# Bias vectors kept in DRAM in 16 copies, read back by eight loads with a step of 511

## The chip, the cores and the metric

The kernel runs on one core of one Trainium2 chip. The metric is the device time of one execution in microseconds (us). All arithmetic is in 32-bit floats; large matrix products are made of three passes over a high and a low part of each operand.

## The reference, cut to what matters

Two transformer blocks follow each other over 256 tokens of width 1024. The first has a mixer of three kinds (differential attention, an RWKV-7 recurrence, attention over a memory) and a mixture of 16 experts. The second has two layers, each with two feed-forward nets of width 2816 around a mixer. In these two layers every attention score gets a bias that depends only on the distance between query and key:

```
bias[h, q, k] = table[bucket(q - k), h]      # 16 heads, masked where q < k
layer 0: heads 0-7 a mixture of dilated windows, heads 8-15 the best keys of an index
layer 1: 16 heads, window of 128, a sink for each head
out = softmax(q k^T / 8 + bias) v
```

So for one head the whole 256 x 256 bias follows from a vector of 512 values: row p of a tile is the vector read from a place that moves by one element for each p (a Toeplitz tile).

## The kernel before, in words

**Weights.** The weights are a stream of slots of 1.5 MB, in the order in which they are used. SyncE (SP) loads each slot in three pieces "a", "b" and "d" of 512 KB into `raw`, which has two slots (L423). ScalarE (ACT) copies a piece to `w_hi` (L536), VectorE (DVE) writes the rest to `w_lo` (L907), and TensorE (PE) multiplies (L1478 to L1480). Piece a or b of slot n may be loaded once slot n-2 has been split, and the order on SP is a(n+1), b(n+1), d(n). ACT and DVE split the pieces in program order among their other work, so a piece that comes late holds what follows it on both engines. All loads of SP use the queue q1.

**Stages.** Slots 0 to 9 are the projections of the first mixer; three slots (OUT0) are its output projection; 64 slots are the experts (`MOE0`); then come a feed-forward net of 22 slots (`FFA0`), the mixer of layer 0 (`HYB0`, attention, three slots `HOUT0`), two feed-forward nets (`FFB0`, `FFC0`), the mixer of layer 1 (`SWA0`, attention, `SOUT0`) and the last net (`FFD0`). Before each of them a norm computes, transposes and splits the activations.

**Bias.** Early on, PE makes two sets of vectors, one for each layer (L1755), and ACT copies them to `vec_sb`, 16 partitions (one for each head) of 2 x 512 floats (L729, semaphore `vec_ready`). GpSimd (POOL) waits until the first mixer's attention has its first scores (L484) and then stores, for each of the two sets, the whole Toeplitz tiles to DRAM: from each of the 16 partitions 128 overlapping rows of 384 floats (L488), 3 MB for each set, to `bias_tiles` (`bias_dram` in the code, shape 2 x 16 x 128 x 384). Before the feed-forward net `FFA0` it loads the first set into `zb`, 128 partitions of 16 x 384 floats (L499); after the attention of layer 0 it loads the second (L514). The waits for `bias_loaded` stand before the attentions that use them. All DMAs of POOL use the queue q0.

```
pool.wait_ge(S_("att_scores"), 1)
for v in range(2):
    row = vec_sb[0:16, v, P - 1:P]
    pool.dma_start(bias_dram[v], bass.AP(row.tensor, row.offset, [list(row.ap[0]), [-1, P], [1, 3 * P]]))
...
pool.dma_start(zb, bias_dram[0].rearrange("h p c -> p h c"))
```

Of the kernel before, what the change touches and what calls it, by code (L numbers as in the profile page):

```python
# [16 lines left out]
F32 = mybir.dt.float32  # L17
# [6 lines left out]
P = 128  # L24
# [68 lines left out]
LAM_INIT = 0.8 - 0.6  # L93
RMS_EPS = 1e-6
TOP_ROUNDS = S // 4 // 8
RW_GN_EPS = 64e-5


def block_program(nc, wstream, x_in, mem_in, pos_in, pos_cols_in, pcol_in, prow_in, smallw_in, const_in, table_in, bias_lookup_in,
                  bias_dram, out):  # L100
    ctx = ExitStack()
    with ctx:
# [5 lines left out]
        def S_(name):  # L108
            if name not in sems:
                sems[name] = ctx.enter_context(nc.semaphore(name))  # L110
            return sems[name]
# [21 lines left out]
        def at(kb, *shape):  # L133

            n = int(np.prod(shape))
            o = int(kb * 256)
            assert o + n <= arena_kb * 256
            v = arena[:, o:o + n]
            names = "abcd"[:len(shape)]
            if len(shape) > 1:  # L140
                v = v.rearrange(f"p ({' '.join(names)}) -> p {' '.join(names)}", **dict(zip(names[1:], shape[1:])))
            return v
# [11 lines left out]
        def cst(name):  # L154
            return part(CONSTS, const, name)
# [109 lines left out]
        zb = at(16, 16, 3 * P)  # L265
# [7 lines left out]
        vec_sb = at(52, 2, 512)  # L273
# [60 lines left out]
        for j in range(2):  # L334
            for t in range(T):
                units.append(dict(kind="mem", t=t, nk=T, q=mqT[:, j], k=mkT[:, j], col=768 + 128 * j,
                                  v=lambda m, kb, j=j: mkv[:, kb, 256 + 128 * j + 64 * m:256 + 128 * j + 64 * m + 64]))
        for kind, qv, kv, vv, col in (("a", h_qaT, h_kaT, h_va, 0), ("b", h_qbT, h_kbT, h_vb, 512)):
            for j in range(4):
                for t in range(T):  # L340
# [3 lines left out]
                                      v=lambda m, kb, j=j, vv=vv: vv[:, kb, 128 * j + 64 * m:128 * j + 64 * m + 64]))  # L344
        for j in range(8):
            for t in range(T):
                units.append(dict(kind="c", t=t, nk=t + 1, q=s_qT[:, j], k=s_kT[:, j // 4], col=128 * j, j=j,
                                  z=zb[:, 2 * j:2 * j + 2, P * (1 - t):P * 2],
                                  v=lambda m, kb, j=j: s_v[:, kb, 64 * (j // 4):64 * (j // 4) + 64]))
# [96 lines left out]
        @block.gpsimd  # L446
        def _(pool):
            def inverse_rms(i):

                pool.wait_ge(S_("ssq_ready"), i + 1)  # L450
                if i:
                    pool.wait_ge(S_("xs_ready"), i)
                    pool.wait_ge(S_("xs1_ready"), i)
                nc.gpsimd.tensor_scalar(meansq, ssq, RMS_EPS, None, ALU.add).then_inc(S_("meansq_ready"), 1)
                pool.wait_ge(S_("meansq_ready"), i + 1)
                nc.gpsimd.tensor_tensor(rstd, meansq, minus_half, ALU.pow).then_inc(S_("rstd_ready"), 1)

            pool.dma_start(tab[0:34, :], table_in).then_inc(S_("tab_loaded"), 16)
            pool.dma_start(oh[0:34], bias_lookup_in).then_inc(S_("tab_loaded"), 16)
            nc.gpsimd.memset(minus_half, -0.5).then_inc(S_("pool_const"), 1)  # L460
            pool.wait_ge(S_("pool_const"), 1)
            inverse_rms(0)
            pool.wait_ge(S_("raw_d0"), 16)
            pool.dma_start(const[:, P:CONSTW], const_in[:, P:CONSTW]).then_inc(S_("const_loaded"), 16)
            at_wq, at_gain = SMALLW["wq"][0], PROW["final_g"][0]
            pool.dma_start(smallw[:, 0:at_wq], smallw_in[:, 0:at_wq]).then_inc(S_("smallw_loaded"), 16)
            pool.dma_start(prow[:, 0:at_gain], prow_in[0:at_gain].partition_broadcast(P)).then_inc(S_("prow_loaded"), 16)
            pool.dma_start(posi[:, 0:S], pos_in[0:1, :].rearrange("a s -> (a s)").partition_broadcast(P)
                           ).then_inc(S_("pos_loaded"), 16)
            pool.dma_start(posi[:, S:S + T], pos_cols_in).then_inc(S_("pos_loaded"), 16)  # L470

            pool.wait_ge(S_("l1t_ready"), 2)
            pool.wait_ge(S_("elem_done"), 1)
            for i, lvl in enumerate(LEVELS[1:]):
                if i >= 2:
                    pool.wait_ge(S_("inv_prod"), 2 * i - 2)
                m = cst("level_t")[:, P * (i + 1):P * (i + 2)].unsqueeze(1).broadcast_to([P, 8, P])
                nc.gpsimd.tensor_tensor(levt[i % 2], l1t, m, ALU.mult).then_inc(S_("lev_ready"), 1)


            pool.wait_ge(S_("inv_mm"), 2 * (len(LEVELS) - 1))
            pool.dma_start(mem_sb[:, :, :], mem_in.rearrange("(t p) d -> p t d", p=P)).then_inc(S_("mem_loaded"), 16)
            inverse_rms(1)
            pool.wait_ge(S_("att_scores"), 1)  # L484
            for v in range(2):

                row = vec_sb[0:16, v, P - 1:P]
                pool.dma_start(bias_dram[v], bass.AP(row.tensor, row.offset, [list(row.ap[0]), [-1, P], [1, 3 * P]])  # L488
                               ).then_inc(S_("vec_stored"), 16)
            pool.wait_ge(S_("att_out"), ATT1[1] // QUAD)  # L490
            pool.dma_start(smallw[:, at_wq:SMALLWS], smallw_in[:, at_wq:SMALLWS]).then_inc(S_("smallw_loaded"), 16)
            pool.dma_start(prow[:, at_gain:PROWS], prow_in[at_gain:PROWS].partition_broadcast(P)).then_inc(
                S_("prow_loaded"), 16)
            for i in (2, 3):
                inverse_rms(i)

            pool.wait_ge(S_("vec_stored"), 32)
            pool.wait_ge(S_("y_added"), 2)
            pool.dma_start(zb, bias_dram[0].rearrange("h p c -> p h c")).then_inc(S_("bias_loaded"), 16)  # L499
            inverse_rms(4)  # L500

            pool.wait_ge(S_("bias_loaded"), 16)
            pool.wait_ge(S_("key_mask"), T)
            for u in range(*ATT3):
                un = units[u]
                w = un["nk"] * P
                if u - ATT3[0] >= 2:
                    pool.wait_ge(S_("att_max"), u - 1)
                nc.gpsimd.tensor_tensor(bz[:, u % 2, :, 0:w], un["z"],
                                        smask[:, un["t"], 0:w].unsqueeze(1).broadcast_to([P, 2, w]), ALU.add  # L510
                                        ).then_inc(S_("att_bz"), 1)
            pool.wait_ge(S_("att_out"), ATT3[1] // QUAD)
            pool.wait_ge(S_("att_bz"), ATT3[1] - ATT3[0])
            pool.dma_start(zb, bias_dram[1].rearrange("h p c -> p h c")).then_inc(S_("bias_loaded"), 16)  # L514
            for i in range(5, sum(n["norm"] for n in norms) + 1):
                inverse_rms(i)

# [2 lines left out]
        def _(act):  # L520
# [254 lines left out]
            for i in range(len(LEVELS) - 1):  # L775
# [12 lines left out]
            act.wait_ge(S_("rw_var"), 1)  # L788
            nc.scalar.activation(rw_st[:, 8:16], rw_st2[:, 0:8], ACT.Sqrt, bias=RW_GN_EPS, scale=1.0 / HD).then_inc(
                S_("rw_gnstd"), 1)  # L790
# [101 lines left out]
        def _(dve):  # L892
# [3 lines left out]
            def link(ins):  # L896

                step[0] += 1
                ins.then_inc(S_("dve_step"), 1)
                dve.wait_ge(S_("dve_step"), step[0])  # L900
# [114 lines left out]
            def attention(u0, u1, rounds=()):  # L1015

                for i in range(u0, u1 + 4):
                    if i < u1:
                        max_unit(i)
                    if u0 <= i - 1 < u1 and units[i - 1]["kind"] == "da":  # L1020
                        combine_unit(i - 1)
                    for r in rounds[2 * (i - u0):2 * (i - u0) + 2] if i < u1 else rounds[2 * (u1 - u0):]:
                        top_round(*r)
                    if i >= u1:
                        rounds = ()
                    if u0 <= i - 4 < u1 and (i - 4) % QUAD == QUAD - 1:
                        out_quad(i - 4)

            def top_round(t, r):
# [5 lines left out]
                link(nc.vector.match_replace(scw[:, 0:w], m8, src, GONE))  # L1035
                if r == TOP_ROUNDS - 1:
                    link(tt(smask[:, t, 0:w], scw[:, 0:w], s_, ALU.is_equal))
# [200 lines left out]
            for g in range(T):  # L1238
                v = invt[:, 4 * g:4 * g + 4]
                tt(v, eye8[:, 0:4], v, ALU.subtract).then_inc(S_("inv_ready"), 1)  # L1240
            for i in range(len(LEVELS) - 1):
                for g in range(T):
                    dve.wait_ge(S_("inv_mm"), 2 * i + g + 1)
                    for mat, bank in ((inv, 2), (invt, 4)):
                        if mat is invt or i < len(LEVELS) - 2:
                            v = mat[:, 4 * g:4 * g + 4].rearrange("p u t -> p (u t)")
# [186 lines left out]
            for t in range(T):  # L1433
# [8 lines left out]
                ins.then_inc(S_("idx_sum"), 1)  # L1442
                dve.wait_ge(S_("idx_sum"), t + 1)
                link(tt(s_, s_, cst("causal")[:, S * t:S * t + w], ALU.add))
            dve.wait_ge(S_("bias_loaded"), 16)
            attention(*ATT2, rounds=[(t, r) for t in range(T) for r in range(TOP_ROUNDS)])
            attention(*ATT3)
            norm(6)
# [6 lines left out]
            norm(9)  # L1455
            for n in range(SWA0, SOUT0):
                proj(n)
            dve.wait_ge(S_("bias_loaded"), 32)
            attention(*ATT4)
            norm(10)  # L1460
            for n in range(SOUT0, FFD0):
# [666 lines left out]
```

## Time and profile before

| what | value |
|---|---|
| time, median of 3 runs | 1711.43 us (1711.15 to 1716.26) |
| time of the profiled execution | 1711.93 us |
| its span | 1710.0 us |
| PE busy | 1577.5 us (92%) |
| DVE busy | 1026.8 us (60%) |
| ACT busy | 811.7 us (47%) |
| POOL busy | 43.6 us (3%) |
| mean rate of all DMA | 180 GB/s |

The profile shows one execution. Busy time is the time in which an engine computes; the span is the time from the first to the last instruction. "DMA share" is the mean busy share of the core's 16 DMA engines. PEclk is the granted clock of TensorE as a share of full speed.

### The profile page before, as it was taken

How to read it: one execution, taken by the hardware profiler on the slowest of the kernel's cores; microseconds unless marked ns; L12 is line 12 of the kernel's file. 1: busy time of each engine (PE TensorE's matmuls, PEld its weight loads, DVE VectorE, ACT ScalarE, POOL GpSimd, SP SyncE). 2: the span in 40 equal slices, each digit the busy share in tenths (PEclk: the TensorE clock that was granted, in tenths of full speed). 3: DMA queues.
4: the chain of work that ended last, by engine and by line, in shares of the span. 5: the costliest groups of instructions: out<-in, count | busy, mean ns of one | idle time of the engine just before them, and what ended most of it. 6: DMA issues, size and time to landing. Idle time of an engine off the chain costs nothing.

```text
span 1710.0 us, 29397 instructions
## 1 busy us (share of the span) xinstructions
PE 1577.5 (92%) x10556; PEld 1436.6 (84%) x10556; DVE 1026.8 (60%) x1564; ACT 811.7 (47%) x1308; POOL 43.6 (3%) x53
## 2 busy tenths in 40 slices
PE   7898774899999999999996999999999999999997
PEld 6788573798888868999895789999899988889997
DVE  5745843598888955555543755555555554655554
ACT  6423432477677744333443454333433345653332
POOL 1120000000000000000000100000000000000000
PEclk9898787899999999999997599999999999999999
DMA  6312694399979966555452055555455544155552
GB/s 248 111 62 78 113 107 141 134 348 348 350 255 352 346 227 222 184 184 184 148 185 74 0 185 194 187 185 186 148 186 186 185 163 149 47 176 185 184 184 74
DMA packets 83846, 308.03 MB, mean 180 GB/s; under 512 B 9278, under 2 KB 9406, under 8 KB 83648
## 3 DMA queue, kind: packets, MB, share of 16 engines
q1 hardware_dynamic: 79632, 289.97, 48.8%
q0 software_dynamic: 3856, 16.98, 5.3%
q8 instruction: 48, 0.79, 0.2%
q14 instruction: 22, 0.18, 0.0%
q10 hardware_dynamic: 288, 0.12, 0.0%
HBM read 299.69 MB, written 7.34 MB: 180 GB/s over the span
## 4 chain that ended last, share of the span: by engine, by line
PE 84%; DVE 8%; ACT 4%; DMA 2%; issue 1%; POOL 0%; SPq 0%; DVEq 0%; POOLq 0%; ACTq 0%
PE ps L1478 24%; PE ps L1479 23%; PE ps L1480 23%; PE ps L1484 3%; PE ps L1607 2%; DMA raw<-in_wstream 2%; DVE w_lo L907 2%; PE ps L1579 1%; PE ps L1667 1%; PE ps L1742 1%; ACT arena L590 1%; DVE xT_lo L946 1%; ACT w_hi L536 1%; ACT xT_hi L609 1%; PE ps L1823 1%
## 5 line engine op out<-in xcount | busy, mean ns | idle before, releaser
L907 DVE TENSOR_TENSOR w_lo<-raw,w_hi 128x1024 fp32r<-128x1024 f32 x549 | 646.6, 1221 | 286.3 <-ACT w_hi L536 284.7
L536 ACT ACTIVATE w_hi<-raw 128x1024 fp32r<-128x1024 f32 x549 | 549.3, 1055 | 240.2 <-PE ps L1480 190.4
L1478 PE MATMUL ps<-xT_hi,w_hi 128*128 128x256 f32 x1656 | 470.5, 284 | 4.5 <-DVE xT_lo L946 3.7
L1479 PE MATMUL ps<-xT_lo,w_hi 128*128 128x256 f32 x1656 | 468.8, 283 | 0.0
L1480 PE MATMUL ps<-xT_hi,w_lo 128*128 128x256 f32 x1656 | 468.8, 283 | 0.0
L1478 PEld LDWEIGHTS ps<-xT_hi,w_hi 128*128 128x128 f32 x1656 | 317.6, 192 | 10.4 <-issue 6.9
L1479 PEld LDWEIGHTS ps<-xT_lo,w_hi 128*128 128x128 f32 x1656 | 317.7, 192 | 3.2
L1480 PEld LDWEIGHTS ps<-xT_hi,w_lo 128*128 128x128 f32 x1656 | 317.7, 192 | 0.0
L1478 PE MATMUL ps<-w_hi,xT_hi 128*128 128x256 f32 (+2 forms) x848 | 263.1, 310 | 21.7 <-DVE w_lo L907 20.1
L1479 PE MATMUL ps<-w_lo,xT_hi 128*128 128x256 f32 (+2 forms) x848 | 252.8, 298 | 0.0
L1480 PE MATMUL ps<-w_hi,xT_lo 128*128 128x256 f32 (+2 forms) x848 | 252.6, 298 | 0.0
L1478 PEld LDWEIGHTS ps<-w_hi,xT_hi 128*128 128x128 f32 x848 | 162.7, 192 | 38.7 <-issue 34.6
L1478 PE MATMUL ps<-w_hi,h_hi 128*128 128x512 f32 x480 | 189.1, 394 | 4.4 <-DVE h_lo L1094 4.4
L1479 PE MATMUL ps<-w_lo,h_hi 128*128 128x512 f32 x480 | 188.8, 393 | 0.0
L1480 PE MATMUL ps<-w_hi,h_lo 128*128 128x512 f32 x480 | 187.2, 390 | 0.0
L1479 PEld LDWEIGHTS ps<-w_lo,xT_hi 128*128 128x128 f32 x848 | 163.0, 192 | 0.1
L1480 PEld LDWEIGHTS ps<-w_hi,xT_lo 128*128 128x128 f32 x848 | 162.7, 192 | 0.0
L651 ACT ACTIVATE arena<-ps 128x256 f32<-128x256 f32 x88 | 33.9, 385 | 251.1 <-PE ps L1480 251.1
L1058 DVE TENSOR_TENSOR h_hi<-ps,arena 128x256 fp32r<-128x256 f32 x88 | 37.3, 423 | 153.6 <-ACT arena L651 153.6
L1484 PE MATMUL ps<-const,arena 128*128 128x128 f32 x416 | 83.7, 326 | 44.5 <-ACT arena L600 14.5
L1484 PEld LDWEIGHTS ps<-const,arena 128*128 128x128 f32 x416 | 57.2, 165 | 64.1 <-issue 25.2
L1480 PEld LDWEIGHTS ps<-w_hi,h_lo 128*128 128x128 f32 x480 | 90.3, 188 | 20.0
(311 smaller groups left out, 1324.9 us busy)
## 6 DMA issues: line engine op xcount, KB each, us to landing
raw<-in_wstream SPq DMA_DIRECT2D x549, 512.0 KB, 5.0
bias_tiles<-arena POOLq DMA_DIRECT2D x2, 3072.0 KB, 51.3
arena<-bias_tiles POOLq DMA_DIRECT2D x2, 3072.0 KB, 14.6
const<-in_const POOLq DMA_DIRECT2D x1, 1112.0 KB, 7.7
x_res<-in_x SPq DMA_DIRECT2D x2, 512.0 KB, 4.3
arena<-in_mem POOLq DMA_DIRECT2D x1, 1024.0 KB, 5.5
out<-arena SPq DMA_DIRECT2D x2, 512.0 KB, 2.7
smallw<-in_smallw POOLq DMA_DIRECT2D x1, 768.0 KB, 39.1
```

Of the source, the lines that this page charges most:

```text
L536: nc.scalar.activation(w_hi[:, slot, lo:hi], raw[:, slot, lo:hi], ACT.Copy).then_inc(S_(f"hi_{part_}"), 1)
L590: ins = nc.scalar.activation(mem_sq[t] if c == 1 else scaled[:, t, :], n["src"][:, t, :], ACT.Square, scale=D ** -0.5, accum_out=ssq[:, t: ...
L609: ins = nc.scalar.activation(xT_hi[:, k, :], turned(c, k), ACT.Copy, scale=n["gain"][:, k:k + 1])
L651: nc.scalar.activation(silu[:, f % 2, :], ps[:, 4 + f % 2, 0:S], ACT.Silu).then_inc(S_("silu_ready"), 1)
L907: tt(w_lo[:, slot, lo:hi], raw[:, slot, lo:hi], w_hi[:, slot, lo:hi].bitcast(F32), ALU.subtract).then_inc(S_(f"lo_{part_}"), 1)
L946: ins = stt(xT_lo[:, k, :], turned(c, k), n["gain"][:, k:k + 1], xT_hi[:, k, :].bitcast(F32), ALU.mult, ALU.subtract)
L1058: tt(h_hi[:, b, :], up, silu[:, b, :], ALU.mult)
L1478: a = mm(out_, stat_[0], mov[0], start=start, stop=False)
L1479: b = mm(out_, stat_[0], mov[1], start=False, stop=False)
L1480: c = mm(out_, stat_[1], mov[0], start=False, stop=stop)
L1484: return nc.tensor.transpose(out_, in_, ident)
L1607: ins = mm(o, pt[:, u % 2, m * nk + kb, :], v, start=kb == 0, stop=kb == nk - 1)
```

## The change

The stored form of the bias is another one, and so are the transfers:

- `bias_tiles` shrinks from 2 x 16 x 128 x 384 floats to 2 x 16 x 16 x 512: each head's vector of 512 floats is stored 16 times, one copy behind the other.
- The two stores (512 KB each instead of 3 MB) are issued as soon as `vec_ready` is there, ahead of POOL's wait for `l1t_ready`. They no longer stand behind `att_scores`.
- Each load of `zb` becomes eight loads, one for each block of 16 partitions. In a block, partition i reads copy i from a place one element further to the left: the step between partitions is 511 floats. A load still brings 16 rows of 384 floats to each partition, so the bytes that arrive in `zb` are as many as before (3 MB a set).
- The waits count eight loads of 16 instead of one.

```diff
+COPIES = 16
+BIAS_LOADED = 16 * (P // COPIES)
@@ gpsimd, after the loads of positions
+            pool.wait_ge(S_("vec_ready"), 1)
+            for v in range(2):
+
+                pool.dma_start(bias_dram[v], vec_sb[0:16, v, :].unsqueeze(1).broadcast_to([16, COPIES, 512])).then_inc(
+                    S_("vec_stored"), 16)
+
+            def load_bias(v):
+
+                for a in range(P // COPIES):
+                    rows = bias_dram[v]
+                    pool.dma_start(zb[COPIES * a:COPIES * a + COPIES], bass.AP(
+                        rows.tensor, rows.offset + P - 1 - COPIES * a,
+                        [[511, COPIES], [512 * COPIES, 16], [1, 3 * P]])).then_inc(S_("bias_loaded"), 16)
+
             pool.wait_ge(S_("l1t_ready"), 2)
@@ gpsimd, after inverse_rms(1)
-            pool.wait_ge(S_("att_scores"), 1)
-            for v in range(2):
-
-                row = vec_sb[0:16, v, P - 1:P]
-                pool.dma_start(bias_dram[v], bass.AP(row.tensor, row.offset, [list(row.ap[0]), [-1, P], [1, 3 * P]])
-                               ).then_inc(S_("vec_stored"), 16)
@@ gpsimd, the two loads
-            pool.dma_start(zb, bias_dram[0].rearrange("h p c -> p h c")).then_inc(S_("bias_loaded"), 16)
+            load_bias(0)
             inverse_rms(4)
 
-            pool.wait_ge(S_("bias_loaded"), 16)
+            pool.wait_ge(S_("bias_loaded"), BIAS_LOADED)
...
-            pool.dma_start(zb, bias_dram[1].rearrange("h p c -> p h c")).then_inc(S_("bias_loaded"), 16)
+            load_bias(1)
@@ vector
-            dve.wait_ge(S_("bias_loaded"), 16)
+            dve.wait_ge(S_("bias_loaded"), BIAS_LOADED)
...
-            dve.wait_ge(S_("bias_loaded"), 32)
+            dve.wait_ge(S_("bias_loaded"), 2 * BIAS_LOADED)
@@ kernel()
-    args.append(nc.dram_tensor("bias_tiles", (2, 16, P, 3 * P), F32, kind="Internal").ap())
+    args.append(nc.dram_tensor("bias_tiles", (2, 16, COPIES, 512), F32, kind="Internal").ap())
```

## Rows read from the trace of the kernel before

**Rows 1.** The page: shares of the span in the chain that ended last, by line.
```profile
PE ps L1478 24%; PE ps L1479 23%; PE ps L1480 23%; PE ps L1484 3%; PE ps L1607 2%; DMA raw<-in_wstream 2%; DVE w_lo L907 2%; PE ps L1579 1%; PE ps L1667 1%; PE ps L1742 1%; ACT arena L590 1%; DVE xT_lo L946 1%; ACT w_hi L536 1%; ACT xT_hi L609 1%; PE ps L1823 1%
```

**Rows 2.** The chain of waits, 225 to 330 us (start, duration, what).
```profile
238.25 3.66 SPq L423
242.23 24.06 DMA raw<-in_wstream
...
268.83 0.55 PE ps L1478
```

**Rows 3.** DMA issues: size, median us to landing; then the bias transfers alone.
```profile
raw<-in_wstream SPq DMA_DIRECT2D x549, 512.0 KB, 5.0
...
L488 POOL DMA_DIRECT2D bias_tiles<-arena x2: 1037/1072/1107, 193.6 to 194.7; - x2
...
DMA to landing us min/median/max: 13.8/25.4/67.2
```

**Rows 4.** Stretches: PE, PEld, DVE, ACT, POOL busy, PEclk, DMA share, GB/s.
```profile
237.00:251.00 14.00, 14.00 (x84) 14.00 (x83) 5.46 (x6) 2.55 (x3) 0.00 (x0) 1.00 0.97 99
251.00:260.00 9.00, 1.38 (x12) 1.17 (x10) 0.00 (x0) 0.00 (x0) 0.00 (x0) 0.69 0.99 161
...
262.00:264.00 2.00, 0.00 (x0) 0.00 (x0) 0.00 (x0) 0.00 (x0) 0.00 (x0) 0.50 1.01 420
```

**Rows 5.** PE in order of time, around the wait in the output projection.
```profile
252.10 0.28 PE L1480 MATMUL ps<-w_hi,xT_lo 128*128 128x256 f32 x1
268.83 0.55 PE L1478 MATMUL ps<-w_hi,xT_hi 128*128 128x256 f32 x1 [16.46 <-DVE w_lo L907]
...
274.73 0.35 PE L1478 MATMUL ps<-w_hi,xT_hi 128*128 128x256 f32 x1
```

**Rows 6.** Weight loads issued at 652 to 657 us, then at 995 to 999 us.
```profile
L423 SPq DMA_DIRECT2D raw<-in_wstream x3: 332/333/333, 652.2 to 653.9; - x3
...
DMA to landing us min/median/max: 6.6/8.0/8.5
...
L423 SPq DMA_DIRECT2D raw<-in_wstream x3: 333/333/333, 995.1 to 996.8; - x3
...
DMA to landing us min/median/max: 8.5/9.1/9.8
```

**Rows 7.** Stretches around the starts of the two loads of the bias.
```profile
646.00:648.00 2.00, 1.94 (x16) 1.73 (x16) 0.40 (x2) 1.27 (x4) 0.28 (x1) 1.00 0.55 65
...
991.00:993.00 2.00, 1.42 (x8) 1.45 (x9) 2.00 (x7) 2.00 (x6) 0.00 (x0) 1.00 0.88 173
```

**Rows 8.** PE and ACT in order of time, where these weights are used.
```profile
671.57 0.28 PE L1478 MATMUL ps<-xT_hi,w_hi 128*128 128x256 f32 x1
...
1006.74 1.06 ACT L536 ACTIVATE w_hi<-raw 128x1024 fp32r<-128x1024 f32 x1 [4.90 <-DMA raw<-in_wstream]
...
1008.30 0.28 PE L1478 MATMUL ps<-w_hi,xT_hi 128*128 128x256 f32 x1
```

**Rows 9.** The early stretch: `vec_sb`, weight loads, and their splits.
```profile
32.20 1.00 ACT L729 ACTIVATE arena<-ps 16x1024 f32<-16x1024 f32 x1
...
L423 SPq DMA_DIRECT2D raw<-in_wstream x3: 332/333/333, 30.3 to 32.0; - x3
...
39.50 2.97 ACT L536 ACTIVATE w_hi<-raw 128x1024 fp32r<-128x1024 f32 x3
...
52.05 2.94 ACT L536 ACTIVATE w_hi<-raw 128x1024 fp32r<-128x1024 f32 x3
...
38.00:42.00 4.00, 4.00 (x36) 4.00 (x35) 3.90 (x10) 3.99 (x8) 0.00 (x0) 1.00 0.02 6
```

**Rows 10.** POOL in order of time.
```profile
78.13 5.74 POOL L478 TENSOR_TENSOR arena<-arena,const 128x1024 f32<-128x1024 f32 x2 [64.05 <-ACT arena L767]
...
989.23 1.23 POOL L514 DMA_DIRECT2D arena<-bias_tiles  x1 [9.84 <-DVE arena L1009]
1017.38 0.22 POOL L454 TENSOR_SCALAR stat<-stat 128x2 f32<-128x2 f32 x1 [26.91 <-ACT arena L590]
```

## Prediction

> **What bounds the kernel now.** I read the page's chain by line first. About seven tenths of it are the three passes of matmuls, which the change does not touch; but 2% is `raw<-in_wstream`, waits for weights [rows 1]. A transfer of the bias competes with the weights for the same 16 DMA engines, so the question is where these 2% lie. The chain in order of time answers it: the largest piece by far is one load of 24.06 us at 242.23, behind an issue on SP that took 3.66 us; the splits on ACT and DVE and then PE follow it [rows 2]. A weight load lands after 5.0 us in the median [rows 3]. At that time the two stores of the bias run: they are issued at 193.6 and 194.7 and the last lands 67.2 us later, at 261.9 [rows 3]. So the stores set the end of a stage. The stretches say how. From 237 to 251 us the DMA engines are full (share 0.97) and yet move only 99 GB/s; with the stores gone they move 420 [rows 4]. The two stores, 6.3 MB in the 66 us from their start to 261.9, make 95 GB/s on their own. Both read 16 partitions. So the weights issued from 237 us on get next to nothing at first: the total stays at 99 GB/s for 14 us, and only then rises to 161 [rows 4]. The reader is to see two facts: a transfer on 16 partitions is slow at a full DMA share, and a weight load behind it first waits until some 14 us x 99 GB/s = 1.39 MB of it have gone, then takes turns with it.
>
> **What the change removes.** PE stops at 252.4 for want of piece d of the third output slot and starts at 268.8, a wait of 16.46 us [rows 5]. After it PE runs at half its clock until 274.7: 27 matmuls of 0.213 us instead of 0.12, so 2.6 us more (the granted clock in the wait is 0.50 [rows 4], the 1.2 GHz level). Without the stores at that time, the load issued at 238.2 lands after 5.0 us, at 243, and ACT and DVE need 2.3 us for the split, so it is there before 252.4. Gain: 16.5 + 2.6 = 19.1 us. The norm, the router and the experts behind it only move ahead.
>
> **The stores, moved.** `vec_sb` is ready at 33.2 [rows 9], so they start at about 35. They hold 1.05 MB, again on 16 partitions: at 97 GB/s, between the 95 and the 99 of the old stores, 10.8 us, to about 46; if they ran at the rate of a full-width transfer, 3 us. Three weight loads are issued at 30.3 to 32.0, ahead of them; they are split from 39.5 to 42.5 (the piece issued last is third), and from 38 to 42 the DMA engines are idle (share 0.02) [rows 9]. That idle time is the cover. If the last piece took turns with the stores from 35 on, its 0.5 MB would need 6.6 us and come at about 42, 0.5 to 1 us late; if it had to wait for all of them, up to 4 us. Being issued first, it should be let through: I take 0.5 us and keep 0 and 4. The later loads (issued from 42.4 on) are split from 52 on [rows 9] and are covered. On POOL nothing waits behind the new wait before the multiplications at 78 us [rows 10].
>
> **The loads of the bias, cut in eight.** The bytes are the same, 3.15 MB a set. POOL issues eight DMAs instead of one; even at the 1.2 to 1.6 us of one large issue, the second set is out 10 to 13 us after 989.2, and the next work there comes at 1017.4 [rows 10]; the attentions that need `zb` come some 300 us (first set) and 200 us (second) later. So the loads cost nothing by themselves. What counts is how long they hold up the weights. Before, one load on 128 partitions lands after 13.8 us (first set) [rows 3], a rate of 228 GB/s, and weights beside it land after 6.6 to 9.8 us instead of 5.0 [rows 6]. Now each load writes 16 partitions, as the old stores read 16. That operation is not in the trace. The bounds: 97 GB/s (nearest in shape) and 228 GB/s (nearest in kind), so 32.5 and 13.8 us a set.
>
> The Trainium skill, "SBUF — State Buffer", section "Door 1: The DMA port swizzle", speaks against the change here: what counts is how many of 16 ports the partitions reach, and partitions 0 to 15 reach 4, with a measured 104 GB/s at 1 MiB. The trace's 99 GB/s agrees for reads; for writes no run here shows it yet. By that rule, applied to all eight one after the other, the sum is that of the first rival below; by the old load's row it is that of the second.
>
> Now the price for a rate r. The eight loads start at 646.5 (half the share of the stretch from 646) and 991.2 [rows 7]. The weights come at 652.2 and 995.1, three loads (1.57 MB) of which the third is the piece d that ACT splits first [rows 6]. They wait for 1.39 MB, take turns for the rest (1/r + 1/400 us per KB of each), and the remainder goes at 400 GB/s; 0.5 us for completion. At the first place d and then a must be split before PE can go on (1.06 us on ACT and twice 1.22 on DVE, 3.5 in all), and PE needs a at 671.6 [rows 8]. At the second one split follows (2.3 us) and PE needs it 15 matmuls after 1008.3, at 1010.4 [rows 8]; ACT already waits 4.90 us for this piece there, so it has no slack left.
>
> - r = 97: 0.55 MB are gone at 652.2; 14.3 us, then 1.21 MB in turns (15.5 us), then 0.9: third piece at 682.9, PE at 686.9, 15.3 late. At the second place 0.38 MB gone, 14.3 + 17.7 + 0.5 us: 1027.6, PE 20.0 late. Two returns from half clock, 2.6 each. Loss 40.5 us.
> - r = 160: 8.7 + 7.4 + 1.8 us: 670.1, PE 2.5 late; 1014.8, PE 7.2 late. Loss 9.7, and 2.6 for one return, after the longer stop.
> - r = 120 and r = 200, in the same way: losses of 28.1 and 5.9 us.
> - r = 228: 664.2, no wait; 1008.9, 1.3 late. The trace has 662.4 and 1006.6 for this case [rows 6], so the working is 2 us late at this end; it holds at the slow end, from which its numbers come. In the middle I take off 1 us for each place.
>
> Which r? The old stores drew on the same 16 partitions all along. The eight loads lie in one queue and write eight different blocks. A DMA engine that ends its part of one block a little early goes on to the next, where it has few rivals; that lead grows from block to block. I take the middle of the bounds, 160 GB/s: loss (2.5 - 1) + (7.2 - 1) + 2.6 = 10.3 us.
>
> **Sum.** -19.1 + 0.5 + 10.3 = -8.3 us on the profiled execution, whose 1711.93 us lie 0.5 above the median (span 1710.0). On the median: 1711.4 - 8.3 = 1703.
>
> **Rivals.**
> 1. *The eight loads run one block after the other at the rate of the stores* (97 GB/s). For it: the nearest row in shape, and all 16 engines have equal parts, so they may stay in step. Against it: stores and loads differ, and here the block changes. -19.1 + 0.5 + 40.5 = +21.9: 1733, slower. The sign turns at r of about 138 GB/s (a set in 23 us). This is the one case on the other side.
> 2. *Sixteen partitions don't matter on the writing side*, the stores were slow for their overlapping reads. For it: the stores are the only slow transfer in the trace and also the only one of that form. Nothing is lost at the loads: -18.6, so 1693.
> 3. *The moved stores hold up the early projections*, where DVE and ACT are on the chain: up to 4 us on top of any case. It decides no sign by itself except near the turn.
> That the change does nothing is excluded by the wait of 16.46 us, unless piece d were late for another reason, and no other transfer runs there.
>
> **How the numbers follow.** Rates of 120 to 200 GB/s (the likeliest case): 48 in 100, 1721 to 1698 (-19.1 + 0.5 and the losses above). Rival 1: 27 in 100. Rival 2: 25 in 100. A measurement of this kernel tells about 0.3% (5 us) from no change. Faster by more is rival 2 and the upper half of the middle case (r above 155): 0.50. Within: r of about 128 to 155, 0.14. Slower: rival 1 and the rest, 0.36. The range reaches over both rivals: 1690 to 1733.
>
> **What would show it.** In the profile after: no weight wait near 242 to 266 and PE through the third output slot at about 256 (gain). Time from the first issue to the landing of the last load of `zb`: 14, 20 or 32 us. ACT's wait for `raw` at 663 (none, 5, 18 us) and at 1006 (5, 11, 25). The DMA share near 1 at 100 GB/s would be rival 1. The prediction is wrong if r is far from 160, or if the weights get through sooner than they did beside the stores.

## The result: slower by 1%

| | time, us |
|---|---|
| before, median of 8 runs | 1710.45 (1707.05 to 1716.26) |
| after, median of 8 runs | 1725.07 (1720.17 to 1739.13) |
| ratio | 1.0097, 95% interval 1.0076 to 1.0117 |
| predicted | 1703 (1690 to 1733) |

The change makes the kernel slower; I had forecast faster. The eight times of after lie in two groups, five from 1720.2 to 1725.1 and three from 1733.9 to 1739.1; the profiled execution (1733.91) is one of the upper three. The two groups have a cause of their own, which comes last below.

**Where the time went.** POOL computes the reciprocal norm before each stage, so its rows are milestones that both traces have. After, from POOL in order of time (the bracket is POOL's idle time, here without meaning):

```profile
257.28 0.22 POOL L456 TENSOR_SCALAR stat<-stat 128x2 f32<-128x2 f32 x1 [32.21 <-ACT arena L600]
618.10 0.22 POOL L456 TENSOR_SCALAR stat<-stat 128x2 f32<-128x2 f32 x1 [359.80 <-ACT arena L600]
619.06 4.90 POOL L484 DMA_DIRECT2D arena<-bias_tiles  x8
827.71 0.22 POOL L456 TENSOR_SCALAR stat<-stat 128x2 f32<-128x2 f32 x1 [203.75 <-ACT arena L600]
979.24 4.51 POOL L484 DMA_DIRECT2D arena<-bias_tiles  x8 [11.74 <-DVE arena L1019]
1024.62 0.22 POOL L456 TENSOR_SCALAR stat<-stat 128x2 f32<-128x2 f32 x1 [40.86 <-ACT arena L600]
1415.90 0.22 POOL L456 TENSOR_SCALAR stat<-stat 128x2 f32<-128x2 f32 x1 [194.72 <-ACT arena L600]
1530.52 0.22 POOL L456 TENSOR_SCALAR stat<-stat 128x2 f32<-128x2 f32 x1 [113.60 <-ACT arena L600]
```

Before, the same milestones (two of them; 989.23 and 1017.38 are in [rows 10]):

```profile
278.84 0.22 POOL L454 TENSOR_SCALAR stat<-stat 128x2 f32<-128x2 f32 x1 [51.68 <-ACT arena L590]
...
1508.45 0.22 POOL L454 TENSOR_SCALAR stat<-stat 128x2 f32<-128x2 f32 x1 [98.81 <-ACT arena L590]
```

The rest are at 643.73, 839.26 and 1408.64. Difference by difference:

| stretch | before | after | change |
|---|---|---|---|
| to the norm after the output projection | 278.84 | 257.28 | -21.6 |
| experts, to the norm before `FFA0` | 364.89 | 360.82 | -4.1 |
| feed-forward net with the first set's loads | 195.53 | 209.61 | +14.1 |
| mixer of layer 0, to the second set's first load | 149.97 | 151.53 | +1.6 |
| `HOUT0` with the second set's loads | 28.15 | 45.38 | +17.2 |
| `FFB0`, `FFC0` | 391.26 | 391.28 | 0 |
| mixer of layer 1 | 99.81 | 114.62 | +14.8 |
| sum to that norm | | | +22.1 |

The profiled executions differ by 1733.91 - 1711.93 = 22.0. The -4.1 shows in no trace of the experiments below (364.3 to 364.9 in each), though seven of them have the same code in this stretch, so it belongs to this one execution. The +1.6 comes and goes too: the mixer of layer 0 takes 149.8 to 150.0 us in some traces and 151.5 to 151.8 in others, of one and the same code. The +14.8 is a matter of the upper group, as shown below. Without the -4.1 and the +14.8, the sum is +11.4, and the lower group stands 10 to 15 us above before.

**The gain is there.** The output projection no longer stops. PE's last matmul of it, in order of time (a row with idle time ahead of it ends in a bracket; this one has none, where PE was idle for 16.46 us before [rows 5]; the norm's work follows at 253.95):

```profile
253.83 0.28 PE L1490 MATMUL ps<-w_hi,xT_lo 128*128 128x256 f32 x1
```

**The loss.** The transfers of the bias, by source line (issue durations in ns, then first and last start; below each set of loads the us from each load's own issue to its landing):

```profile
L477 POOL DMA_DIRECT2D bias_tiles<-arena x2: 574/578/582, 33.4 to 34.0; - x2
...
L484 POOL DMA_DIRECT2D arena<-bias_tiles x8: 563/563/983, 619.1 to 623.4; - x8
...
DMA to landing us min/median/max: 6.2/16.2/30.8
...
L484 POOL DMA_DIRECT2D arena<-bias_tiles x8: 563/563/621, 979.2 to 983.2; - x8
...
DMA to landing us min/median/max: 5.9/16.5/29.1
```

One load of all 3 MB landed after 13.8 us [rows 3]. Now the last of eight, issued at 623.4, lands 30.8 us later, 35 us after the first issue. Meanwhile the DMA engines are full and move little. Stretches, the first of them from the kernel before while its one load runs, the others from after (columns as in [rows 4]):

```profile
648.00:658.00 10.00, 9.38 (x77) 9.39 (x78) 7.88 (x15) 6.87 (x11) 0.00 (x0) 1.00 0.99 371
```

```profile
625.00:630.00 5.00, 5.00 (x43) 4.99 (x43) 2.92 (x5) 1.89 (x4) 0.00 (x0) 1.00 1.03 109
630.00:635.00 5.00, 5.00 (x43) 4.96 (x42) 4.15 (x5) 2.46 (x4) 0.00 (x0) 1.00 1.03 114
640.00:645.00 5.00, 5.00 (x37) 4.70 (x36) 0.00 (x0) 0.00 (x0) 0.00 (x0) 1.00 0.99 162
650.00:655.00 5.00, 0.00 (x0) 0.00 (x0) 0.00 (x0) 0.05 (x1) 0.00 (x0) 0.50 0.99 233
985.00:990.00 5.00, 5.00 (x30) 5.00 (x30) 3.04 (x3) 1.40 (x2) 0.00 (x0) 1.00 1.05 118
```

It is the picture of [rows 4] again, with writes into SBUF in place of reads: 99 GB/s then, 109 to 118 now. The traffic by queue says the same: from 625 to 635 us only q0, POOL's queue, moves anything (0.55 and 0.57 MB in 5 us each). The weights, issued on q1 from 627 on, get their first bytes at 637, and then both queues move about as much (0.39 and 0.42 MB from 640 to 645, 162 GB/s together). The chain of waits goes through one weight load at each place, and PE's row says what it costs (the second fence is PE in order of time):

```profile
627.70 0.33 SPq L425
628.27 26.60 DMA raw<-in_wstream
654.95 1.06 ACT w_hi L546
...
987.11 0.33 SPq L425
987.69 24.77 DMA raw<-in_wstream
1012.54 1.06 ACT w_hi L546
```

```profile
658.55 0.55 PE L1488 MATMUL ps<-xT_hi,w_hi 128*128 128x256 f32 x1 [12.43 <-DVE w_lo L917]
...
1015.00 0.55 PE L1488 MATMUL ps<-w_hi,xT_hi 128*128 128x256 f32 x1 [13.85 <-DVE w_lo L917]
```

The number in the bracket is PE's idle time: 12.4 and 13.9 us. After it PE starts at the lower level of its clock, 1.2 GHz (the granted clock from 650 to 655 us is 0.50).

**The two groups.** Stretches of the last attention, after and then before:

```profile
1460.00:1480.00 20.00, 19.90 (x90) 16.23 (x91) 9.07 (x20) 10.90 (x42) 0.00 (x0) 0.51 0.00 0
```

```profile
1450.00:1470.00 20.00, 18.75 (x147) 14.79 (x147) 15.99 (x37) 16.23 (x64) 0.00 (x0) 1.00 0.00 1
```

In this execution PE runs this part, 430 us after the stop at 1015, at half its clock: 90 matmuls in 20 us instead of 147.

### The profile page after: what moved, and what is told of

Read it like the earlier page. It is cut to its first block, busy times and chain, and to the rows that moved or that the text cites. A ratio compares the mean times of both kernels' runs of the same rounds, so it can differ in the third digit from the quotient of the medians.

```text
span 1732.1 us, 29411 instructions
## 1 busy us (share of the span) xinstructions
PE 1590.7 (92%) x10556; PEld 1449.1 (84%) x10556; DVE 1026.9 (59%) x1564; ACT 812.5 (47%) x1308; POOL 49.2 (3%) x67
## 4 chain that ended last, share of the span: by engine, by line
PE 82%; DVE 8%; ACT 4%; DMA 3%; issue 1%; POOL 0%; DVEq 0%; SPq 0%; POOLq 0%; ACTq 0%
PE ps L1488 23%; PE ps L1489 23%; PE ps L1490 23%; DMA raw<-in_wstream 3%; PE ps L1494 3%; PE ps L1617 2%; DVE w_lo L917 2%; PE ps L1589 2%; DVE xT_lo L956 1%; PE ps L1677 1%; ACT w_hi L546 1%; ACT arena L600 1%; PE ps L1752 1%; ACT xT_hi L619 1%; PE ps L1833 1%
## 5 line engine op out<-in xcount | busy, mean ns | idle before, releaser
L1488 PE MATMUL ps<-xT_hi,w_hi 128*128 128x256 f32 x1656 | 471.6, 285 | 16.4 <-DVE w_lo L917 12.4
L1488 PEld LDWEIGHTS ps<-xT_hi,w_hi 128*128 128x128 f32 x1656 | 318.5, 192 | 22.8 <-issue 19.3
L1494 PE MATMUL ps<-const,arena 128*128 128x128 f32 x416 | 89.2, 343 | 44.3 <-ACT arena L610 14.4
L1494 PEld LDWEIGHTS ps<-const,arena 128*128 128x128 f32 x416 | 60.7, 175 | 66.3 <-issue 28.4
L1488 PEld LDWEIGHTS ps<-w_hi,h_hi 128*128 128x128 f32 x480 | 90.7, 189 | 19.3 <-DVE h_lo L1104 4.7
## 6 DMA issues: line engine op xcount, KB each, us to landing
arena<-bias_tiles POOLq DMA_DIRECT2D x16, 384.0 KB, 16.2
```

The costliest lines, as they stand in the source:

```text
L1488: a = mm(out_, stat_[0], mov[0], start=start, stop=False)
L1494: return nc.tensor.transpose(out_, in_, ident)
```

## The experiments

Times are medians; "set" is the 3 MB of bias of one layer, the first place is the feed-forward net `FFA0`, the second `HOUT0`. The comparison is the kernel before, run again beside each experiment (1712.0 to 1712.4 us). The first four ask what makes the loads slow: the 16 neighbouring partitions (theory), the reads at odd addresses that the step of 511 makes (rival), or the number of DMAs (rival). They also take the gain by itself.

**1. The stores alone.** Kernel before, with the stores of the change and one 128-partition load a set, which reads its rows from the weights (the values of the bias are others, the bytes are the same):

```diff
+            pool.wait_ge(S_("vec_ready"), 1)
+            for v in range(2):
+                rows = bias_dram[v]
+                pool.dma_start(bass.AP(rows.tensor, rows.offset, [[16 * 512, 16], [512, 16], [1, 512]]),
+                               vec_sb[0:16, v, :].unsqueeze(1).broadcast_to([16, 16, 512])).then_inc(
+                    S_("vec_stored"), 16)
...
-            pool.wait_ge(S_("att_scores"), 1)
-            for v in range(2):
...
-            pool.dma_start(zb, bias_dram[0].rearrange("h p c -> p h c")).then_inc(S_("bias_loaded"), 16)
+            pool.dma_start(zb, bass.AP(
+                wstream.tensor, wstream.offset, [[16 * 6 * P, P], [6 * P, 16], [1, 3 * P]])).then_inc(S_("bias_loaded"), 16)
```

> The kernel before with the stores of the change alone: 16 copies of 2 KB for each head, issued at vec_ready; each set of zb still comes in one load on 128 partitions. The load reads 16 rows of 384 floats for each partition from the weight stream instead of the bias, so the bias values are not the reference's; bytes, rows and target are those of before. This prices the gain. Theory (the gain is the wait behind the old stores, 19.1 us, with a few us more from the stages around it): the stretch up to the first load of zb ends 20 to 26 us earlier and that stays to the end, 1685 to 1692 us, 0.985 to 0.989 of before. Rival (the moved stores cost something in the early projections): 4 us less gain, 1690 to 1695.

Measured: 1690.36 us against 1712.19, as expected, ratio 0.9864 (0.9844 to 0.9884). The norms stand at 257.76, 622.50, 818.06 and 996.16: 21.1 us are gained in the first 258 us and all of them are still there at each later norm. The stores land 10.2 us after issue in the median and delay nothing in the early projections.

**2. The eight loads alone.** Kernel before, whose tiles of aligned rows are read by eight loads of 16 neighbouring partitions:

```diff
+            def load_bias(v):
+                for a in range(8):
+                    pool.dma_start(zb[16 * a:16 * a + 16], bias_dram[v, :, 16 * a:16 * a + 16, :].rearrange(
+                        "h p c -> p h c")).then_inc(S_("bias_loaded"), 16)
...
-            pool.dma_start(zb, bias_dram[0].rearrange("h p c -> p h c")).then_inc(S_("bias_loaded"), 16)
+            load_bias(0)
... (the second set and the counts of the waits likewise)
```

> The kernel before with the loads of zb alone cut into eight blocks of 16 neighbouring partitions, read from the full Toeplitz tiles; the stores stay as before. Rows are 1536 bytes at multiples of 1536 bytes, no step of 511. Theory (16 neighbouring partitions take writes at about 105 to 115 GB/s, and the weights queue behind): the last of eight loads lands some 30 us after the first issue, PE waits 13 to 20 us at each of two places, and the time is 1738 to 1746 us (1.017 to 1.021). Rival (the step of 511 and its odd addresses make the loads slow): the loads land within 16 us, time as before, 1710.

Measured: 1757.38 us, 1.0243 (1.0208 to 1.0278). One of the four runs (1745.0) lies in the expected range; the other three (1756.3 to 1760.7) are above it, and the traced one of them has the long last attention of the upper group (117.2 us against 99.8), which the expectation left out. The slowest load of each set lands after 29.9 and 30.3 us; the net with the first set takes 209.1 us instead of 195.5. The step of 511 isn't needed for the loss, and neither are the copies.

**3. The same number of loads on partitions eight apart.**

```diff
-                    pool.dma_start(zb[COPIES * a:COPIES * a + COPIES], bass.AP(
-                        rows.tensor, rows.offset + P - 1 - COPIES * a,
-                        [[511, COPIES], [512 * COPIES, 16], [1, 3 * P]])).then_inc(S_("bias_loaded"), 16)
+                    pool.dma_start(zb[a:P:P // COPIES], bass.AP(
+                        rows.tensor, rows.offset + P - 1 - a,
+                        [[512 - P // COPIES, COPIES], [512 * COPIES, 16], [1, 3 * P]])).then_inc(S_("bias_loaded"), 16)
```

> The changed kernel with one difference: the eight loads of a set write the partitions a, a+8, a+16, ... instead of 16 neighbours, and read with a step of 504 between partitions instead of 511. As many DMAs, rows, bytes and copies; the same values in zb. Theory (it matters which partitions a DMA touches: 16 neighbours share few ways into the memory, 16 spread ones reach twice as many): a set lands in 15 to 19 us at about 200 GB/s, the waits for weights at the two places shrink from 20 us to at most 5, and the time is 1690 to 1702 us (0.988 to 0.995 of before). Rival (16 partitions in a DMA, or eight DMAs instead of one, or reading at odd addresses is what costs): as the changed kernel, 30 us a set, 1720 to 1725.

Measured: 1707.52 us, 0.9961 (0.9932 to 0.999), again in two groups: six runs from 1693.8 to 1702.4, as expected, and six from 1712.6 to 1716.2. Bytes, number of loads and odd addresses are those of the change; only which partitions a load writes is another. Stretches at both places, and the loads:

```profile
632.00:637.00 5.00, 5.00 (x44) 5.00 (x43) 2.87 (x6) 1.89 (x3) 0.00 (x0) 1.00 1.04 210
978.00:983.00 5.00, 5.00 (x31) 5.00 (x30) 2.49 (x4) 2.01 (x2) 0.00 (x0) 1.00 1.02 213
```

```profile
L484 POOL DMA_DIRECT2D arena<-bias_tiles x8: 560/560/617, 969.6 to 973.5; - x8
...
DMA to landing us min/median/max: 4.4/9.6/17.7
```

The rate at a full share is near twice that of the change. The first place costs nothing (195.55 us), the second 6.4, with PE idle for 4.17 us.

**4. A step of 512.** The change, reading at addresses that are multiples of 256 bytes (so the values of the bias are others):

```diff
-                        rows.tensor, rows.offset + P - 1 - COPIES * a,
-                        [[511, COPIES], [512 * COPIES, 16], [1, 3 * P]])).then_inc(S_("bias_loaded"), 16)
+                        rows.tensor, rows.offset + 64 * (a % 2),
+                        [[512, COPIES], [512 * COPIES, 16], [1, 3 * P]])).then_inc(S_("bias_loaded"), 16)
```

> The changed kernel with the loads reading at a step of 512 floats from the start of each copy (every row starts at a multiple of 256 bytes) into the same blocks of 16 neighbouring partitions; the shift is left out, so the bias values are not the reference's. Theory (the partitions written decide): as the changed kernel, 29 to 31 us a set, 1718 to 1725. Rival (reads at odd addresses cost a seventh more or make the loads slow): a set in 26 us or less, and the time 5 to 25 us shorter.

Measured: 1724.83 us, 1.0098 (1.0064 to 1.0133), the ratio of the change itself. The rate too, as its stretch shows:

```profile
632.00:637.00 5.00, 5.00 (x44) 5.00 (x43) 2.88 (x6) 1.94 (x3) 0.00 (x0) 1.00 1.03 117
```

That settles the first question for the addresses: they cost nothing that shows. Experiment 3 shows that the block of 16 neighbours costs half of the rate; that the number of loads doesn't matter is shown by experiment 6, where four loads run at the rate of the eight of experiment 3. The next four ask by which repair the loss goes away, and whether the copies were needed for the gain.

**5. 32 copies, four loads, every fourth partition.** On top of the edit of experiment 3:

```diff
-COPIES = 16
+COPIES = 32
```

> The changed kernel with 32 copies instead of 16 (stores of 1 MB a set, from 16 partitions as before) and four loads a set instead of eight, each to the partitions a, a+4, a+8, ..., read with a step of 508. Theory (what counts is where the partitions of one DMA lie; every fourth one reaches all the ways that 128 do): a set lands in 13 to 16 us as the one load of the kernel before did, nothing waits for weights at the two places beyond what it did, the moved stores (21 us from 35) cost 0 to 6 us in the early projections; 1688 to 1697 us (0.986 to 0.992). Rival (fewer than 128 partitions in a DMA is slow in proportion): 32 partitions as eight blocks of 16 spread ones at best, 18 us a set and PE late at the second place, 1695 to 1700 without low clock in the last attention.

Measured: 1693.67 us, 0.9884 (0.9867 to 0.9901). The slowest load lands 9.1 and 10.6 us after its own issue, the whole set 11.5 and 12.6 us after the first issue (13.8 and 15.4 us with the single load of before). Both places are free (195.54 us against 195.53 before, 29.1 against 28.15). The loads move 376 GB/s, with nothing on the weights' queue in this stretch:

```profile
630.00:635.00 5.00, 5.00 (x43) 4.98 (x43) 3.51 (x6) 2.06 (x3) 0.00 (x0) 1.00 1.03 376
```

**6. 32 copies, blocks of 32 neighbours.** The edit of experiment 5 alone, in the kernel of the change; the blocks are then four of 32 neighbours.

> The changed kernel with COPIES = 32 and nothing else: four loads of 32 neighbouring partitions a set, step 511. Theory (32 neighbours reach as many ways as 16 partitions at a step of 8): a set in 16 to 19 us, PE not late at the first place and 4 to 8 us late at the second, as with the step of 8. Rival (only the number of partitions in a DMA counts): as the 32 spread ones, both 13 to 16 or both 17 us.

Measured: 1713.67 us, 0.9991 (0.9962 to 1.0021), two runs at 1697.4 and 1697.8 and eight from 1710.1 to 1718.8. The rate is that of 16 partitions eight apart, and so, nearly, is the loss (nothing, then 7.2 us, with PE idle for 3.71):

```profile
632.00:637.00 5.00, 5.00 (x44) 5.00 (x43) 2.87 (x6) 1.89 (x3) 0.00 (x0) 1.00 1.04 203
```

**7. The old stores, early.** Kernel before with its two 3 MB stores moved; no copies, the single loads stay.

```diff
+            pool.wait_ge(S_("vec_ready"), 1)
+            for v in range(2):
+                row = vec_sb[0:16, v, P - 1:P]
+                pool.dma_start(bias_dram[v], bass.AP(row.tensor, row.offset, [list(row.ap[0]), [-1, P], [1, 3 * P]])
+                               ).then_inc(S_("vec_stored"), 16)
...
-            pool.wait_ge(S_("att_scores"), 1)
-            for v in range(2):
-                row = vec_sb[0:16, v, P - 1:P]
-                pool.dma_start(bias_dram[v], bass.AP(row.tensor, row.offset, [list(row.ap[0]), [-1, P], [1, 3 * P]])
-                               ).then_inc(S_("vec_stored"), 16)
```

> The kernel before with its two full Toeplitz stores (3 MB each) issued at vec_ready instead of att_scores; form, size and loads as before. Theory (a transfer on 16 partitions holds up all weights issued behind it, wherever it is): the stores run from 35 to 101 us, the weight loads of 42 us land at 65 or later instead of 49, ACT and DVE wait for them and PE loses 10 to 30 us there, so that the 21 us gained later are mostly or wholly lost: 1700 to 1720 us. Rival (the early projections leave the DMA engines idle most of the time, so moving the stores is all that is needed): 1690 us as with the small stores.

Measured: 1717.5 us, 1.0029 (1.0018 to 1.0039). The wait in the output projection goes, but the early projections pay for it. ACT in order of time:

```profile
78.34 1.06 ACT L537 ACTIVATE w_hi<-raw 128x1024 fp32r<-128x1024 f32 x1 [24.38 <-DMA raw<-in_wstream]
```

The norm that comes at 138.48 us before comes at 162.46. So moving the stores is no gain without making them small.

**8. The loads of the change, paced.** Each of the eight waits for one more tile of the feed-forward net to be multiplied, and the second set waits until behind the norm of `HOUT0`:

```diff
+                    pool.wait_ge(S_("d_used"), (FFA0, FFB0)[v] + 1 + a)
...
+            inverse_rms(5)
             load_bias(1)
```

> The changed kernel with its loads unchanged in form (16 neighbours, step 511) but issued one at a time: load a of the first set waits for the down projection of tile a of the first feed-forward net (d_used at FFA0 + 1 + a), the second set for those of FFB0, behind inverse_rms(5). Theory (the loss is the weights' wait behind some 1.4 MB of slow transfer in the queue): a single load of 0.4 MB takes 3.6 to 4 us, a weight load lands at most that much later, which the 8.5 us of a tile cover; no wait at either place, 1686 to 1694 us (0.985 to 0.991). Rival (the slow transfers cost DMA time however they are spread: 29 us a set in a stretch where the weights need about half of the engines): PE is late by a few us in each of 16 tiles, 1700 to 1725.

Measured: 1693.53 us, 0.9884 (0.9867 to 0.99). The norms from 624.26 on (819.80, 1000.79, 1196.33) show no loss in the two nets (195.5 us each). From 819.80 to 1000.79 it takes 2.9 us more than in experiment 1, but no load of the bias runs there, and experiment 5 has the same 181 us. A single load still takes as long as the first of the change's (6.2 us), but only 0.4 MB of the bias is in front of a weight load at a time. The rival, that the slow transfers cost the same however they are spread, is refuted:

```profile
L485 POOL DMA_DIRECT2D arena<-bias_tiles x16: 566/566/641, 644.4 to 1080.1; - x16
...
DMA to landing us min/median/max: 5.5/6.3/7.7
```

The last three are about the upper group: does the slow DMA bring the half clock in the last attention, or PE's stop at the second place?

**9. A stop without any DMA.** Kernel before; PE waits in the third slot of `HOUT0` for a chain of 17 multiplications on POOL:

```diff
+            for i in range(17):
+                pool.wait_ge(S_("gap"), i)
+                nc.gpsimd.tensor_tensor(at(66, 896), cst("level_t"), cst("level_t"), ALU.mult).then_inc(S_("gap"), 1)
...
+                if n == FFB0 - 1:
+                    pe.wait_ge(S_("gap"), 17)
```

> The kernel before with an artificial stop: behind the second load of the bias POOL runs 17 multiplications of 128x896 into unused memory (a semaphore after each), and PE waits for the last of them ahead of the third slot of the layer-0 output projection. No DMA differs. All values are those of before. This asks what a stop of PE at the second place costs in all. Theory A (a stop costs its length and the slow restart, no more): PE stops at 1008.3 until some 1027, and every time is 1728 to 1734 us, in one group. Theory B (the low clock seen in the layer-1 attention of the changed kernel, 14.7 us in some of its executions, comes with any stop at the second place): times in two groups, 1728 to 1734 and 1743 to 1749, or all in the upper one. Rival to B (the low clock comes with the eight small loads themselves): one group, as in A.

Measured: 1752.39 us, 1.0229 (1.0207 to 1.0252). PE in order of time, then stretches of the last attention:

```profile
1027.36 0.58 PE L1481 MATMUL ps<-w_hi,xT_hi 128*128 128x256 f32 x1 [19.66 <-POOL arena L517]
```

```profile
1470.00:1490.00 20.00, 18.97 (x90) 14.84 (x90) 10.86 (x24) 12.23 (x44) 0.00 (x0) 0.55 0.02 6
1490.00:1510.00 20.00, 20.00 (x88) 15.91 (x88) 8.15 (x18) 8.99 (x35) 0.00 (x0) 0.50 0.01 1
```

The stop costs 21.9 us where it stands, and the last attention takes 118.4 us instead of 99.8: another 18.6. Together 40.5, the whole loss (1752.4 less 1712.0). All five runs (1745.3 to 1755.9) fit the upper group of theory B; four are above its range, as the last attention takes 18.6 us more where 14.7 were assumed. No transfer differs from before, so no slow DMA is needed. That the chain on POOL itself, and not PE's stop, lowers the clock later was not tested; the change and experiments 2, 3 and 6 have the low clock without that chain, and the stop is what they share with this run.

**10. Only the first set as in the change**, the second one behind the norm and paced:

```diff
+                    if v == 1:
+                        pool.wait_ge(S_("d_used"), FFB0 + 1 + a)
...
+            inverse_rms(5)
             load_bias(1)
```

> The changed kernel with the first set's eight loads as they are and the second set paced (one load for each tile of FFB0, behind inverse_rms(5)). The loss at the first place alone. Theory: 14 us over the paced kernel, 1704 to 1710 us (0.996 to 0.999 of before), in one group, with no low clock in the layer-1 attention, if that comes with the stop at the second place.

Measured: 1706.74 us, 0.9961 (0.9944 to 0.9979), in one group. PE is idle for 13.30 us at the first place, which costs 16.2 us (211.8 against 195.5); the second costs nothing, and the last attention takes 99.8 us.

**11. Only the second set as in the change**, the first one paced:

```diff
+                    if v == 0:
+                        pool.wait_ge(S_("d_used"), FFA0 + 1 + a)
```

> The changed kernel with the first set paced (one load for each tile of FFA0) and the second set's eight loads as they are. The loss at the second place alone. Theory: 17 us over the paced kernel, 1707 to 1712 us, and, if the low clock of the layer-1 attention comes with the stop at this place, a second group of executions at 1722 to 1727. Rival (the low clock comes with the first place's stop, or with neither): one group.

Measured: 1709.37 us, 1.0013 (0.9984 to 1.0041): eight runs from 1704.1 to 1710.8, four at 1724.5 to 1725.5. The second place costs 17.35 us (45.5 against 28.15). The traced run is one of the lower eight: PE is idle for 15.68 us at the second place, and yet the last attention takes 99.9 us. So the stop brings the second group, but not in every execution.

## Why the prediction was wrong

**The gain: right.** Predicted 19.1, measured 21.1 to 21.6 (experiment 1 and the change), all of it kept to the end. Between the norms at 138 and after the output projection, where the gain lies, the three traces with the late stores take 140.1 to 140.4 us and the ten without them 119.5 to 121.1, so 19 to 21 us; the rest lies before the norm at 138, which comes at 137.3 to 138.9. The difference to 19.1 goes with TensorE's clock in the first mixer's attention. In the traced execution of before, the granted clock from 215 to 220 us is 0.50. In experiment 9, with the same late stores, it is 1.00 there, and PE only waits longer for the weights (18.12 us instead of 16.46). Without the stores nothing hides it: 119.7 us in experiment 1 (clock 1.00), 121.1 in experiment 8 (0.50), which is 19.3 below before.

**The early stores: right.** I took 0.5 us and kept 4; experiment 1 shows no loss. Rival 3 is refuted for these stores; experiment 7 shows what six times the bytes do there.

**Eight issues on POOL: right.** 4.5 to 4.9 us for a set, nothing waits for them.

**The rate: the step that failed.** The prediction let the DMA engines run ahead from one block of 16 partitions to the next ("that lead grows from block to block. I take the middle of the bounds, 160 GB/s"). No such lead shows: the measured rate is 109 to 118 GB/s, near the lower bound, at shares of 1.03 to 1.05, and it does not rise before the weights take their turns. So the term for the two places, 10.3 us in the sum, measured 14.1 + 17.2 = 31.3 us. Why the engines gain no lead is open. The prediction chose between its bounds by an argument that no row carried, where its nearest row in shape (97) was 11 to 18% below the truth. The upper bound was not a rate either: 228 GB/s is 3.15 MB over the whole 13.8 us from issue to landing, start included, and once the old load ran, the engines moved 371 GB/s. So the middle between the two was no middle of rates. The first rival, a set in 32.5 us, is near the 35 measured.

The Trainium skill, "SBUF — State Buffer", section "Door 1: The DMA port swizzle", says that the rate follows how many of 16 ports the partitions reach, and gives, for transfers of 1 MiB, 104 GB/s for partitions 0 to 15 (4 ports), 189 for 0 to 31 (8 ports) and 328 for all 128. The runs agree, also for spread partitions, for which it gives no figure: by its formula 16 neighbours reach 4 ports, 16 partitions eight apart or 32 neighbours reach 8, every fourth of 128 reaches 16, and the rates are 109 to 118, 203 to 213 and 376 GB/s. The last step is less than a doubling. The prediction cited this rule against the change and then gave it 27 in 100.

**The price for a given rate: right.** Between its losses of 40.5 us (r = 97) and 28.1 (r = 120), r = 112 gives 32.4 on a straight line; the two places cost 14.1 + 17.2 = 31.3. With it the same sum is -19.1 + 0.5 + 32.4 = +13.8, 1725 us. That this is the measured median is partly luck: 2 us more gain stand against a share of executions with the half clock later, which the sum hasn't got. One part was off: the weights waited until 1.39 MB of the bias had gone in the prediction, and until about 1 MB had gone here (9 us at 109 to 114 GB/s). Experiments 3 and 6 (203 to 213 GB/s) pay nothing at the first place and 6.4 to 7.2 at the second, for which the prediction had 5.9 in all at 200. The sign is shown to turn somewhere between 118 GB/s (slower) and 203 to 213; no run tested the 138 GB/s. And at 203 to 213 the half clock of the next paragraph still takes the gain away in more than half of the executions (14 of 22).

**Not in the prediction at all: the half clock in the last attention.** The traces show it directly in one execution each of the change and of experiments 2, 3, 6 and 9; for the executions without a trace it is read from the time, which then lies in the upper group. Counted so, it comes in no execution of before, nor in experiments 1, 5, 7, 8 and 10, none of which stops PE at the second place; it comes in 3 of 8 of after, 3 of 4, 6 of 12, 1 of 4, 8 of 10 and 4 of 12 in experiments 2, 3, 4, 6 and 11, and in 5 of 5 in experiment 9. It costs 14.8 to 18.6 us when it comes. The stop need not be long. In the traces PE is idle at the second place for 3.71 us in experiment 6 (8 of 10) and 4.17 in experiment 3 (6 of 12), but for 15.55 and 15.68 us in experiments 4 and 11, whose traced executions have no slow last attention. That a stop there, without any change of a transfer, is enough is shown by experiment 9; what links the two over some 430 us is open, and so is what makes it come in one execution and not in the next.

## What to carry to other kernels

When a transfer is cut into blocks of partitions, ask which partitions a piece touches before how many bytes it has: take them spread over all 128 (here every fourth: 376 GB/s against 109 to 118 for 16 neighbours), or, where they have to be neighbours, issue the pieces one at a time between the loads that the main engine waits for. Both repairs turned the loss of 1% into a gain of 1.2%. Half a repair is not enough: at 203 to 213 GB/s the wait shrinks to about 4 us, and the half clock later can still cost 15. And where one row of the trace has the shape of the unknown operation, let it set the value, and leave the middle of the bounds to cases where none does.

## What the runs showed of the hardware that was not expected

- A stop of PE, of 3.7 to 19.7 us here, can be paid twice: where it stands, and again in an attention some 430 us later (99.8 us becomes 114.6 to 118.4), at a granted clock of 0.50 to 0.55.
- The step of 511 floats, with reads at addresses that are no multiple of 256 bytes, is not slower than one of 512 (109 to 118 against 117 GB/s, times 1725.07 and 1724.83 us).
- Four loads of 0.8 MB, each on 32 partitions four apart, move data as fast as one load of 3 MB on all 128 partitions (376 GB/s against 371, both at a full DMA share).
- Weights issued on another queue behind a slow transfer get nothing at all at first (from 627 to 637 us at the first place, while POOL's queue moves 109 to 114 GB/s), and then about half.
